# Prompt attention of a hybrid decoder step: compressed keys in a pair of their own, or in one pair with the local keys

## What is computed

```python
def nsa_block(q, qpos, g, kc, vc, cpos, ks, vs, ov, kw, vw, wpos, tb):
    dc = qpos[:, None] - cpos[None, :]
    lc = jnp.einsum('bthgd,bnhd->bhgtn', q, kc).astype(jnp.float32) * scale
    lc = lc + jnp.transpose(tb[t5_bucket(dc)], (2, 3, 0, 1))
    pc = masked_softmax(lc, dc >= 0)
    oc = jnp.einsum('bhgtn,bnhd->bthgd', pc.astype(vc.dtype), vc)
    ...                                   # ps, osl: the same over the selected tokens
    lw = jnp.einsum('bthgd,bshd->bhgts', q, kw).astype(jnp.float32) * scale
    lw = lw + jnp.transpose(tb[t5_bucket(dw)], (2, 3, 0, 1))
    pw = masked_softmax(lw, (dw >= 0) & (dw < WINDOW) & (wpos[None, :] >= 0))
    ow = jnp.einsum('bhgts,bshd->bthgd', pw.astype(vw.dtype), vw)
    return g[..., 0:1] * oc + g[..., 1:2] * osl + g[..., 2:3] * ow

def fox_block(q, qpos, cq, k, v, ck, kpos):
    l = jnp.einsum('bthd,bshd->bhts', q, k).astype(jnp.float32) * scale
    l = l + jnp.transpose(cq, (0, 2, 1))[..., None] - jnp.transpose(ck, (0, 2, 1))[:, :, None, :]
    p = masked_softmax(l, kpos[None, :] <= qpos[:, None])
    return jnp.einsum('bhts,bshd->bthd', p.astype(v.dtype), v)
```

## Time and profile before

| | |
|---|---|
| three runs | 2428.31, 2429.06, 2429.27 us; median 2429.06 |
| span of the profiled execution | 2428.4 us |
| prompt attention in it | 339.8 to 744.9 us, 405.1 us |
| busy there | PE 380.0, DVE 275.7, ACT 244.3, POOL 191.4 us |

### The profile page before, as it was taken

The page is one execution under the profiler, slowest core; times in us unless marked ns, Lnnn a source line. Parts: engine busy times, 40 slices in busy tenths (PEclk is TensorE's granted clock), DMA queues, the critical chain, the costliest instruction groups (busy, mean ns, idle before and its releaser), DMA issues.

```text
span 2428.4 us, 30908 instructions
## 1 busy us (share of the span) xinstructions
PE 2369.9 (98%) x10983; PEld 1532.6 (63%) x10983; DVE 1236.0 (51%) x3115; ACT 547.6 (23%) x1328; POOL 834.1 (34%) x874
## 2 busy tenths in 40 slices
PE   8999999999998999999999999999999999999999
PEld 4544665555556777688886458888888874443343
DVE  4876716776773444522322794433334324229765
ACT  0001016666663333111111221111011110001131
POOL 0000004554454000475753453334333227203531
PEclk9999999999999999999999999999999999999999
DMA  5423830021018887632325301111111115543201
GB/s 185 106 82 86 273 113 20 1 81 59 1 57 226 234 232 199 209 87 78 87 73 156 83 31 53 36 36 53 35 46 42 36 48 202 175 143 135 84 18 57
DMA packets 185956, 240.28 MB, mean 99 GB/s; under 512 B 53436, under 2 KB 128834, under 8 KB 184266
## 3 DMA queue, kind: packets, MB, share of 16 engines
q1 hardware_dynamic: 181018, 218.99, 29.4%
q10 hardware_dynamic: 1168, 9.58, 1.3%
q0 software_dynamic: 3616, 9.73, 1.2%
HBM read 216.18 MB, written 37.99 MB: 105 GB/s over the span
## 4 chain that ended last, share of the span: by engine, by line
PE 56%; DVE 2%; ACT 1%; issue 0%; DVEq 0%; ACTq 0%
PE ps L2218 36%; PE ps L2382 11%; PE ps L2271 5%; PE ps L2439 2%; PE ps L2369 1%; DVE xT L153 1%; PE ps L2447 1%; ACT xT L2492 0%; PE ps L2275 0%; DVE arena L2970 0%; ACT arena L2589 0%; DVE stats L2644 0%; PE ps L2314 0%; DVE queries L2973 0%; DVE arena L1364 0%
## 5 line engine op out<-in xcount | busy, mean ns | idle before, releaser
L2218 PE MATMUL ps<-xT,arena 128*128 128x272 f32 x1920 | 472.7, 393 | 1.3 <-DVE arena L1375 1.3
L2218 PEld LDWEIGHTS ps<-xT,arena 128*128 128x128 f32 x1920 | 363.9, 190 | 77.0 <-DVE arena L1375 1.7
L2218 PE MATMUL ps<-queries,arena 128*128 128x272 f32 x1312 | 332.6, 393 | 1.8 <-DVE queries L2785 1.0
L2218 PEld LDWEIGHTS ps<-queries,arena 128*128 128x128 f32 x1312 | 249.6, 190 | 54.1 <-DVE queries L2785 1.4
L236 PE MATMUL ps<-arena,xT 128*128 128x512 f32 (+1 forms) x512 | 198.0, 549 | 2.1 <-DMA arena<-in_w_in 1.3
L1008 POOL TENSOR_SCALAR arena<-arena,gates 128x55 f32<-128x55 f32 (+15 forms) x192 | 123.2, 652 | 176.6 <-DVE arena L907 176.4
L943 ACT ACTIVATE arena<-arena 128x640 f32<-128x640 f32 (+15 forms) x256 | 164.7, 643 | 69.0 <-DVE arena L899 49.1
L236 PEld LDWEIGHTS ps<-arena,xT 128*128 128x128 f32 x512 | 97.7, 191 | 102.0 <-issue 93.0
L2218 PE MATMUL ps<-arena 128*128 128x272 f32 x576 | 148.6, 394 | 0.0
L798 PE MATMUL ps<-ident,arena 128*128 128x128 f32 (+4 forms) x880 | 137.8, 284 | 11.0 <-POOL arena L1008 5.2
L786 PE MATMUL ps<-arena,queries 64*128 64x512 f32 (+11 forms) x704 | 128.8, 465 | 14.2 <-DVE arena L899 11.4
(11 more groups left out here) (345 smaller groups left out, 3275.8 us busy)
## 6 DMA issues: line engine op xcount, KB each, us to landing
arena<-in_cache_fox_kv SPq DMA_DIRECT2D x72, 256.0 KB, 4.3
arena<-in_w_ffn_down SPq DMA_DIRECT2D x68, 256.0 KB, 3.3
arena<-in_w_in SPq DMA_DIRECT2D x16, 1024.0 KB, 5.3
xT<-in_w_ffn_down SPq DMA_DIRECT2D x64, 256.0 KB, 3.9
xT<-in_cache_fox_kv SPq DMA_DIRECT2D x56, 256.0 KB, 6.2
arena<-in_cache_nsa_kv SPq DMA_DIRECT2D x64, 192.0 KB, 7.8
arena<-in_w_ffn_up SPq DMA_DIRECT2D x11, 1024.0 KB, 5.4
arena<-in_w_ffn_gate SPq DMA_DIRECT2D x11, 1024.0 KB
```

Source lines behind the costliest of these rows:

```text
L2218: mm = pe.matmul(ps[:, first + BANK_OF[z], 0:PIECE], weight[:, j, :], moving[:, j, :], start=(j == 0 and z in (1, 6, 5, 7)), stop=(j == kk ...
```

## The change

CMP pairs are gone. The compressed keys of a head pair become a second *part* of its WIN pair: they are scored right behind the window's keys into the same place in PSUM, get logits, exponential, sum, inverse and gate of their own, and are turned as one more tile in the same chunks. A tile has six pairs, `ORDER` is (SLC 0, SLC 1, WIN 0, WIN 1, FOX 0, FOX 1), and there are 96 pairs. `normed` and `logits_done` are now counted by parts. The WIN pair of tile 3 (512 + 31 keys) becomes wide. Probabilities have no fixed places: `prob_places` lays them out by size in three rooms. In `TILE_ORDER` tiles 4 and 7 change places. SP's reloads wait for the WIN pairs.

```diff
-            self.slot = (6 * done + 2 * big + j) % 3
-            self.buf = (3 * done + big) % 2
...
+        self.parts = [(branch, 0, self.width)]
+        if branch == WIN:
+            self.parts.append((CMP, self.width, 8 * i + 7))
+        self.all = sum(w for _, _, w in self.parts)
+        self.buf = self.group % 2
+        self.freed = self.group - 1
+        self.tiles = [(branch, self.k0 // P + t, s, w) for t, (s, w) in enumerate(split(self.width, P))]
+        self.tiles += [(b, 0, s, w) for b, s, w in self.parts[1:]]
+        self.wide = self.all > 512
         self.chunks = split(len(self.tiles), 4)
-TILE_ORDER = (6, 0, 5, 1, 4, 2, 3, 7)
+TILE_ORDER = (6, 0, 5, 1, 7, 2, 3, 4)
-ORDER = ((CMP, 0), (SLC, 0), (SLC, 1), (WIN, 0), (CMP, 1), (WIN, 1), (FOX, 0), (FOX, 1))
+ORDER = ((SLC, 0), (SLC, 1), (WIN, 0), (WIN, 1), (FOX, 0), (FOX, 1))
...
+def prob_places():
+    live, places = [], []
+    for p in PAIRS:
+        live = [x for x in live if x[0] > p.n - AHEAD - 1]
...
             for turn in range(2):
+                for j in range(2):
+                    if turn:
+                        sp.wait_ge(logits_done, parts_until(pair_no(0, LAST_TILE, WIN, j)))
+                        slc_bias(sp, at, io, turn, slc_in, j)
+                    for half in range(2):
+                        sp.dma_start(bias_win[:, half, j, :], ...).then_inc(win_in[j], 16)
...
-            sp.wait_ge(logits_done, 2 * pair_no(1, LAST_TILE, CMP, 1) + 2)
+            sp.wait_ge(logits_done, parts_until(pair_no(1, LAST_TILE, WIN, 1)))
             compressor_weights(sp, ahead, io, keep.cw_in)
-            sp.wait_ge(logits_done, 2 * pair_no(1, LAST_TILE, WIN, 1) + 2)
             for p in range(4):
                 key_pages(sp, ahead, io, keep.first_ids, 0, p, keep.k_in)
...
             def scores(p):
...
-                pieces = split(p.width)
+                pieces = [(b, first + s, s, w) for b, first, width in p.parts for s, w in split(width)]
...
+                    if p.branch == WIN:
+                        _, s, w = p.parts[1]
+                        first = T - P + 31 - p.i * P
+                        bias = bias_slc[:, half, p.j, first:first + 16 * (w - 1) + 1:16]
+                        nc.vector.tensor_tensor_reduce(probs_of(p, half, s, w), scores_at(p, half, s, w), bias, -1.0, FLOOR, ALU.add, ALU.min,
+                                                       part).then_inc(logits_done, 1)
...
             def exps(p, half):
+                for part, (b, s, w) in enumerate(p.parts):
+                    act.wait_ge(logits_done, parts_until(p.n, half, part))
...
                 for half in range(2):
+                    for part, (b, s, w) in enumerate(p.parts):
+                        x = probs_of(p, half, s, w)
...
+                        nc.gpsimd.tensor_scalar(x, x, sums[:, p.n % 4, part, half:half + 1], gate, ALU.mult, ALU.mult).then_inc(normed, 1)
```

More of the change, by code:

```diff
@@ L135, in query_weights, with slc_bias @@
     eng.dma_start(query_place(keep, FOX, g), w_in[:, :, C_FQ + g * P:C_FQ + (g + 1) * P]).then_inc(keep.wf_in[g], 16)
[L138 to L142, removed]
+def slc_bias(eng, at, io, turn, there, j):
+    for half in range(2):
+        eng.dma_start(at.bias_slc[:, half, j, :], bias_tile(io, half * NG + 2 * turn + j, False, P - T, P, T)).then_inc(there[j], 16)
 PIECES = ((0, 512), (512, 800), (800, 1312), (1312, W_N))
@@ L658, with parts_until @@
 TURNED_BEFORE = [sum(len(q.chunks) for q in PAIRS[:n]) for n in range(NPAIR + 1)]
+PARTS_BEFORE = [sum(2 * len(q.parts) for q in PAIRS[:n]) for n in range(NPAIR + 1)]
 FOX_SPLITS = [sum(q.branch == FOX and q.i > 0 for q in PAIRS[:n]) for n in range(NPAIR + 1)]
+def parts_until(n, half=1, part=None):
+    p = PAIRS[n]
+    return PARTS_BEFORE[n] + half * len(p.parts) + (len(p.parts) if part is None else part + 1)
+PROB_ROOMS = ((0, 6400), (6400, 1024), (7424, 800))
+def prob_places():
+    live, places = [], []
+    for p in PAIRS:
+        live = [x for x in live if x[0] > p.n - AHEAD - 1]
+        for half in range(2):
+            fits = []
+            for room, (first, size) in enumerate(PROB_ROOMS):
+                if room == 1 and p.n < AHEAD:
+                    continue
+                for a in [first, first + size - p.all, *(b + w for _, b, w in live), *(b - p.all for _, b, _ in live)]:
+                    if first <= a and a + p.all <= first + size and all(a + p.all <= b or b + w <= a for _, b, w in live):
+                        fits.append((-room, a))
+            live.append((p.n, min(fits)[1], p.all))
+        places.append((live[-2][1], live[-1][1]))
+    return places
+PROB_PLACES = prob_places()
 TURN_BANKS = (4, 5, 7)
@@ L707, in probs_of @@
         def probs_of(p, half, s=0, w=None):
-            return (probs_cmp if p.branch == CMP else probs)[:, p.slot, half, s:s + (p.width if w is None else w)]
+            a = PROB_PLACES[p.n][half]
+            (first, _), room = next(x for x in prob_rooms if x[0][0] <= a < sum(x[0]))
+            a += s - first
+            return room[:, a:a + (p.width if w is None else w)]
         def turned_of(p):
-            return (probsT_cmp if p.branch == CMP else probsT)[:, p.buf]
+            return probsT[:, p.buf]
         block = local.enter_context(nc.Block())
@@ L846, in _ @@
             pe.wait_ge(keep.wf_in[NG - 1], 16)
-            scores(PAIRS[0])
-            scores(PAIRS[1])
-            last_queries(0)
-            scores(PAIRS[2])
-            last_queries(1)
-            last_queries(2)
+            for b in range(AHEAD):
+                scores(PAIRS[b])
+                last_queries(b)
             pe.wait_ge(queries_a, 1)
@@ L855, in _ @@
             for p in PAIRS:
-                if p.n == 1:
-                    pe.wait_ge(queries_a, 2)
                 turn(p, 0)
@@ L880, in logits @@
                     dst = probs_of(p, half)
-                    low = nmax[:, p.n % 4, half, 0:1]
+                    low, part = (nmax[:, p.n % 4, half, x:x + 1] for x in range(2))
                     if p.branch == FOX:
                         first = p.width - P
-                        part = nmax[:, p.n % 4, half, 1:2]
                         if first:
```

129 lines of the change are left out of this document (56 added, 73 removed).

## The result

The changed kernel takes 2398.94 us (median of 4 runs, 2395.69 to 2400.91), the kernel before 2429.16 beside it: a ratio of 0.9872 with a 95% interval of 0.9859 to 0.9884, 30.2 us less.

What follows compares the result with a forecast made beforehand. PE's own program, with many small waits on other engines and switching costs, was taken as the bound. From 2429.06: 6.4 + 7.9 + 1.4 + 2.9 - 3.2 - 2.1 - 1.0 = 12.3 us saved, forecast 2417, range 2403 to 2428.

Steps and rivals of the forecast that it cites:

- Steps 1 and 3: PE's compressed-key work, merged with the window's: scoring saves 6.4 us (4.2 to 9.3), values save 1.4 us.
- Step 2: PE's 64 transposes of compressed probabilities cost what the other 816 do: 7.9 us saved, bounds 5 and 9.8.
- Step 4: DVE loses 32 inversions and 28 copies, ACT 28 copies; neither is at its limit: costed at nothing.
- Step 5: PE's waits for logits before scoring shrink by a quarter: 2.9 us saved; bounds 8.5 more saved or 6 lost.
- Step 6: New PE wait for POOL, scaling a merged pair's second half later: 3.2 us lost at eight places, 0 to 13.
- the merged pair is late at POOL: Rival: in 16 wide-tile merged pairs POOL finishes up to 1.5 us later, 24 us lost, 2438; chance 0.10.
- Step 7: FOX's values on PE wait for ACT's later save of NSA sums: six places, 2.1 us lost, or 0.
- Step 8: At the stage's end, later loads of next-stage weights and raw pages make PE wait: 1 us lost, 0 to 4.
- Step 9: Granted clock: one slow stretch more or less is 1.1 us either way; none taken.
- More comes off: Rival: POOL and ACT always in time, logits waits go by their upper bound: 26 us saved, 2403; chance 0.16.

Runs made afterwards that it cites:

- Experiment 9: The kernel before, with one small unused POOL operation (2 columns) ahead of the normalisations of each half, 256 in all: 2447.07 us, ratio 1.0080.
- experiment 2: The kernel before with four pairs ahead instead of three, the changed kernel's tile order and probabilities placed by size; compressed pairs stay separate: 2435.83 us, ratio 1.0019.
- 12: The kernel of experiment 2 (four pairs ahead) plus the small unused POOL operation ahead of its 256 normalisations: 2433.76 us, ratio 1.0020.
- experiment 8: The kernel before with only the tile order changed, to 5, 6, 0, 2, 1, 3, 7, 4 (small tiles together): 2422.66 us, ratio 0.9975.
- experiment 10: The changed kernel with the small unused POOL operation ahead of the normalisations of each half, 192 in all: 2399.67 us, ratio 0.9891.
- experiment 6: The changed kernel with the compressed keys scored in a round of their own again, one more pass through the score places: 2422.16 us, ratio 0.9968.
- Experiment 5: The changed kernel with the compressed tile turned and copied in a block of its own again: 2407.80 us, ratio 0.9911.
- experiment 7: The changed kernel with compressed keys both scored in their own round and turned in their own block; inverses and normalising stay merged: 2437.91 us, ratio 1.0035.
- experiment 4: The changed kernel with its small tiles together, tile order 5, 6, 0, 2, 1, 3, 7, 4: 2391.12 us, ratio 0.9831.

## Why the prediction was wrong

By these runs the stage before ran against two limits at once. One is POOL: a pair has to be scaled before PE turns it, and of the three pairs ahead one or two could be compressed pairs, whose scores keep PE for 0.34 us and whose turning for 0.42, while DVE, ACT and POOL get as many operations for them as for a wide one. Experiment 9 shows that more work on POOL costs time there. The other is the score places: each pair, large or small, has to pass through one of two, and scores wait until logits have left it. Experiments 2 and 12 together show that taking the first away alone gains nothing: POOL has room, and the time stays. That the score places are what holds it then is read from the waits of experiment 2. The other way round is different: in experiment 8, by the tile order alone, the waits for logits halve with POOL as late as before, and 6.0 us are gained. The change moved both in one stroke. It made all three pairs ahead whole, which gave POOL its room (experiment 10), and took 32 of 128 passes through the score places away, which is worth 16 to 23 us in the form of experiment 6. The missing fourth corner, fewer passes with POOL still late, was not tried, so how the 30 us divide between the two stays open.

By the steps:

- **Steps 1 and 3 (scoring, values).** Scores 10.3 us of busy time less, against 6.4 with an upper bound of 9.3; values 1.8 against 1.4. The mechanism was right. Some of the excess of 3.9 us lies with scores that were not touched: the busy time of the 512-key group fell by 0.7 us (640 to 635 ns each), that of 384 keys by 0.5 (528 to 514 ns), as where the clock is a little higher. The rest lies with the compressed scores, as far as these rows go, which step 1 then priced a little too low. Before, then after:

```profile
L786 PE MATMUL ps<-arena,queries 64*128 64x512 f32 x272 | 75.3, 640 | 11.4 <-DVE arena L899 10.7 <-DVE arena L889 0.4
L786 PE MATMUL ps<-arena,queries 64*128 64x384 f32 x80 | 18.0, 528 | 0.0
```
```profile
L816 PE MATMUL ps<-arena,queries 64*128 64x512 f32 x272 | 74.6, 635 | 14.0 <-DVE arena L924 9.4 <-DVE arena L917 2.2 <-DVE arena L930 1.0
L816 PE MATMUL ps<-arena,queries 64*128 64x384 f32 x80 | 17.5, 514 | 0.0
```

- **Step 2 (turning), mis-sized in its effect, not in its price.** 7.9 us were expected; the turning's busy time fell by 14.1. Experiment 5 gives the merged block's own worth: 8.9 us of the kernel's time, 10.1 of the stage, 6.0 of it busy time of the turning (129.73 us there). The step's price holds within some 2 us. The other 8 us of busy time step 2 had not seen. At most 1.4 of them can be the clock, 0.99 to 1.00. By the rows the rest are transposes of full key tiles whose loads waited for POOL, in the group that it took as the normal price ("the 816 others"): 27.5 of the 30.4 us of these waits stand ahead of full tiles (the loads' row of the kernel before, first below), and in experiment 5, with as many turning blocks, 3.3 us of the waits are left (its turning's busy time, and the longer of two rows of the loads' waits, stand behind).

```profile
L798 PEld LDWEIGHTS ps<-ident,arena 128*128 128x128 f32 x816 | 86.1, 140 | 53.7 <-POOL arena L1008 27.5 <-issue 19.1 <-DVE xT L915 3.4
```
```profile
338.20:721.60 383.40, 129.73 (x880) 92.67 (x880) 1.00 0.17 57
```
```profile
PEld ps L830 <- POOL arena L1041: 3.0, 8, 0.6
```

- **Step 4 (off the path).** DVE's 18.2 us less were costed at nothing. No run takes back the inversions alone; experiment 7 keeps them merged and has lost the whole gain, so they alone do not make it.
- **Step 5 (logits).** 2.9 us were to go; nothing did, 12.3 to 12.6 us. The row that the prediction named reads 9.4, near the 9 that it wanted, but those of FOX and of the compressed keys took up the difference. By the rows under experiment 4 what is left stands where a wide tile follows a small one, and the order of that experiment took nearly all of it away (0.8 us left).
- **Step 6 (POOL), wrong in sign: the step that failed.** It found no slack at tile 5's first WIN pair and priced eight such places at 3.2 us lost. The place was well read: PE does wait there, 0.26 us at 408.79 (shown under experiment 4). The fault was to argue from one place, with the pairs ahead as they were, when the change takes the small pairs out of those that run ahead: PE's waits for POOL fell from 5.2 to 0.9 us, its loads' from 30.4 to 4.2. That more work ahead does this is borne out by experiment 2, where the fourth pair ahead alone brought the loads' waits to 7.6. With the step falls the rival of the same root, "the merged pair is late at POOL", and its 2438 us: a POOL with more to do is felt by 18.4 us in the kernel before and by 0.7 in the merged one, or 4.6 by the ratios. The Trainium skill (Perfetto Trace Analysis, section Optimizing Scalar/DVE Operations) says that, where ScalarE and VectorE aren't saturated but hold other engines up, breaking up instructions may let the work finish sooner. The smaller hand-offs are those of the kernel before, and it is the slower one, 2429.16 against 2398.94 us; no run here breaks up a single instruction.
- **Step 7 (`nsa_saved`).** 2.1 us lost were expected; FOX's values went from 38.25 to 38.29 us, with one wait for ACT's save of 0.6 at one place, where six were priced. That is near the lower bound, nothing.
- **Step 8 (the ends).** PE waits 3.46 us for the raw page, 0.75 more, where 1.0 was taken.

```profile
733.33 4.09 PE L1595 MATMUL ps<-ident,arena 128*128 128x128 f32 x20 [3.46 <-DMA arena<-in_cache_nsa_kv]
```

- **Step 9 (the clock).** Not taken; the stage's clock went from 0.99 to 1.00, some 4 us at most; they are part of the busy times above, not beside them.

By the prediction's own measure, the distance from the start of one group to the start of the next, which takes in the wait behind it, 20.1 of the stage's 31.9 us went from the turning and 9.2 from the scores (the expectation of experiment 5 has these numbers). Steps 2, 5 and 6 together gave the turning 7.9 + 2.9 - 3.2 = 7.6 us, step 1 gave the scores 6.4. So the gap is mainly in the turning, 12.5 us, of which step 6 had the sign wrong and step 2 had taken the waits for POOL as part of a normal price; 2.8 us more are in the scores, and 2.1 were never lost at step 7. PE's waits for ACT's copies in the turning went too, from 3.4 us to 0.4; the earlier trace rows shows 0.4 of them ahead of one short group, so step 2's price has them.

"More comes off" named the right side, for its POOL and ACT in time, but it stopped at no loss, where the waits of the kernel before could become a gain, and it looked for the rest in the logits' waits, which stayed.

## What to carry to other kernels

In a software pipeline that counts how far it runs ahead in work items, small items can be expensive: each takes a full place in that lead and a full pass through the shared buffers. Here merging them into a neighbour was worth 30.2 us, where their own blocks on PE had been priced at 15.7 (steps 1 to 3). A wait that the profile puts down to one engine may hide another behind it, as four pairs ahead showed, so price a limit by loading it (a small unused operation on the suspected engine cost one run and told more than the table of waits), and test a cure for one limit together with the other. And where wide and narrow stages share two buffers, keep like beside like: that was worth 6 to 8 us here in either kernel.

## Not expected of the hardware

- POOL, busy for 47% of the stage, cost a third of every microsecond added to it (53.9 us of work, 18.4 us of time): in the changed kernel, where it is busy for 190.6 of 373.3 us, 51%, the added work cost next to nothing. The busy share alone did not tell the two apart.
- The granted clock can fall behind a stretch of waits, and need not. In experiment 7 PE waits for logits twice between tile 1 and tile 7 of the second turn (0.81 and 1.45 us); of the 10 us in which that falls it is busy for 7.62, and the next 10 come at 0.57 of the full clock, so mostly at 1.2 GHz, though PE is busy in them:

```profile
640.00:650.00 10.00, 7.62 (x44) 3.65 (x42) 6.54 (x19) 5.99 (x13) 2.60 (x4) 0.92 0.01 2
650.00:660.00 10.00, 9.39 (x52) 6.24 (x48) 5.20 (x17) 4.01 (x12) 4.31 (x4) 0.57 0.00 0
```

In the changed kernel PE is busy for 7.09 of such 10 us, and the clock stays at 1.00 there and behind:

```profile
570.00:580.00 10.00, 7.09 (x48) 3.72 (x48) 6.74 (x25) 5.54 (x15) 2.65 (x4) 1.00 0.00 0
580.00:590.00 10.00, 9.44 (x72) 5.74 (x70) 8.13 (x28) 7.97 (x23) 7.66 (x10) 1.00 0.01 2
```

What decides between the two these rows do not show. The changed kernel's stage kept 1.00 throughout, where the stage before has 0.99, some 4 us of full clock, so a saving in waits can return a little more than the waits.
